# Sums of weight blocks on GpSimd replaced by accumulating DMAs, and the order of the token-half sums changed

## Chip, cores and metric

One core of a Trainium2 chip runs the kernel. The metric is the device time of one execution in microseconds (us); of several runs the median counts. HW below is 512 columns of fp32, half a weight unit of 128x1024; such a half over 128 partitions is 256 KB.

## What is computed

One step of a trunk of four layers over 640 tokens (512 of group ii and 128 of group i), width 1024, all fp32. Each layer is a token mixer (short convolution, pooling, attention, short convolution) followed by a SwiGLU feed-forward with hidden width 2816:

```python
def swiglu(h, w_in, w_out):
    g, u = jnp.split(h @ w_in, 2, axis=-1)
    return (jax.nn.silu(g) * u) @ w_out
...
        xp = xp + mod_p[5] * swiglu(hp, ffn_in_w[i], ffn_out_w[i])
        xs = xs + mod_s[5] * swiglu(hs, ffn_in_w[i], ffn_out_w[i])
```

## The kernel before

**Precision.** Every fp32 product is made of three fp32r ones: a value is kept as a high and a low part, and PE (TensorE) adds hi x hi, hi x lo and lo x hi. ACT (ScalarE) makes the high part of a weight unit by a copy to w_hi (line 1203; line 1253 for half units), DVE (VectorE) the low part by subtracting it from the raw weights (line 1701; line 1821). The order of work is written out by hand on each engine, with semaphores between them.

**Loads.** SP (SyncE) loads weight units of 128x1024 into the four rows of `raw`, one DMA of 512 KB each (line 443), as soon as the low part of the unit that lay there is made. POOL (GpSimd) loads modulation weights in layers 0 to 2 by its own DMA queue (line 542), none in layer 3.

**The feed-forward of layer 3.** The hidden tiles are taken in chunks of 8, 8 and 6. A hidden tile needs one gate unit and one up unit: a pair. In layers 0 to 2, and for the first two pairs of layer 3, a unit is multiplied plainly (lines 704, 705; `h_unit`, `ffn_in_quad`). For the other 6 + 8 + 6 = 20 pairs of layer 3 `seven_chunk` is used: tokens are halved (320 and 320 columns, two more for the shift), the feature dimension is halved, and gate and up make the third split, so eight half-size products are due; seven are made instead (Winograd's form of Strassen's scheme), of sums of weight blocks and sums of token halves. One product p1 to p7 is 4 feature tiles x 3 passes = 12 matmuls of 128x322 (line 757). Products come in the order of `_order`: p1, p5, p2, p6, p3, p7 for the first pair, then p1 of the next pair, p4 of the last, p5, p6, p2, p7, p3. After a chunk the 8 output units of the down projection follow (lines 704, 705).

**Block homes.** w_hi and w_lo hold four half units; a block is split into the home of the block four (at a few places three) before it, once the product of that one is through (`REFILL`). So ACT's `refill` (block_hi, line 1253) stands directly behind its wait for a product: in `after_p5` ahead of the copy out of PSUM that PE's p3 waits for (p5_kept, line 1299), in `after_p1` and `after_p6` behind the copies that p6 and p7 wait for (p1_kept, line 1292; u2_kept, line 1303). On DVE `after_p3` adds p3 (line 1883), multiplies by rinv (line 1886) and splits a block, `after_p7` adds p7 (line 1904), for which PE's p4 waits (c22_out).

**Sums of weight blocks.** POOL makes four a pair with tensor operations (`s13`, `s2`, `s4`; lines 591, 595, 601, 608). Blocks 1, 2 and 4 are halves of the raw weights; 5 is the sum s1 in s1_home, which is row 2 of tmp; 7, 6 and 3 are differences that overwrite halves of `raw` in place, so POOL waits until DVE has made the low part of block 1 (line 595) and of block 2 (line 608) of that pair.

**Sums of token halves.** POOL makes them once, for four feature tiles k = 0 to 3: t1_of (lines 556 to 558) and t234_of (lines 566 to 571). ACT and DVE split them: `t1_hi_of`, `t2_hi_of` (line 1266), `t3_hi_of` (line 1269), `t4_hi_of` (line 1274), and t1_lo (line 1834), t2_lo (line 1840), t3_lo (line 1844), t4_lo (line 1848). The order on POOL is t1 of all k, t234 of k = 0 and 1, then s13 and s2 of the first pair, and between s2 and s4 of it t234 of k = 2 and 3. On ACT and DVE the splits of t2 are spread over the four units of the plain quad (`T2_ROWS`), and those of t3 follow at the start of `seven_chunk`.

**Around the first product.** In the last plain quad, `ffn_in_quad` takes a unit out of PSUM (line 1775 bias copy, line 1777 product with rinv), multiplies by the gate (line 1788), and ACT makes the high part of the hidden row (line 1215), DVE the low one (line 1715). The first four blocks of a chunk are split within units 2 and 3 of it (`first_blocks`).

```python
def after_p1(p):
    act.wait_ge(product_ready, r + p - 1)
    done(p, 1)
    act.activation(gate_row(p)[:, 0:TA], bank_x(p)[:, 0:TA], ACT.Copy).then_inc(p1_kept, 1)
    refill(p, 1)
def after_p5(p):
    done(p, 5)
    refill(p, 5)
```

Of the kernel before, what the change touches and what calls it, by code (L numbers as in the profile page):

```python
# [18 lines left out]
F32 = mybir.dt.float32  # L19
# [153 lines left out]
def build(nc, d):  # L173
    with ExitStack() as ctx:
# [99 lines left out]
        s_made = sem("s_made")  # L274
# [118 lines left out]
        s1_home = tmp[:, 2, 0:HW]  # L393

        def block_source(p, m):

            j = 2 * (p % 2)
            return {1: raw[:, j, 0:HW], 6: raw[:, j, 0:HW], 2: raw[:, j, HW:2 * HW], 3: raw[:, j, HW:2 * HW],
                    7: raw[:, j + 1, 0:HW], 4: raw[:, j + 1, HW:2 * HW], 5: s1_home}[m]
# [21 lines left out]
        def _(sp):  # L421
# [17 lines left out]
            def load(q, tiles, units=range(4)):  # L439
                for j in units:  # L440

                    sp.wait_ge(w_lo_ready, 4 * q + (j - 3))
                    sp.dma_start(raw[:, j, 0:tiles * P], d["weights"][4 * q + j, :, 0:tiles * P]).then_inc(raw_in[j], 16)

# [35 lines left out]
            for layer in range(DEPTH):  # L480
# [33 lines left out]
                with sp.Fori(0, 2 * (Q_IN + Q_OUT)) as i:  # L514
                    load(i + q, KD)
                q += 2 * (Q_IN + Q_OUT)
                with sp.Fori(0, Q_LAST) as i:
                    load(i + q, KD)
                q += Q_LAST
# [11 lines left out]
        def _(pool):  # L531
# [45 lines left out]
            def s13(layer, c, p, q, n):  # L577

                first, j, qq = _pairs_before(layer, c), 2 * (p % 2), q + p // 2
# [3 lines left out]
                if p == 0 and c == 0:  # L583

                    pool.wait_ge(sum_ready, 2 * layer + 2)
                elif p:

                    pool.wait_ge(block_lo_ready, SEVEN * first + PLACE[n][p - 1, 5] + 1)
                elif c > FIRST_SEVEN[layer]:
                    pool.wait_ge(block_lo_ready, SEVEN * first)  # L590
                pool.tensor_tensor(s1_home, up_w[:, 0:HW], up_w[:, HW:2 * HW], ALU.add).then_inc(s_made, 1)

                pool.wait_ge(block_lo_ready, SEVEN * first + PLACE[n][p, 1] + 1)
                pool.wait_ge(s_made, 4 * (first + p) + 1)
# [2008 lines left out]
```

## Time and profile before

| | |
|---|---|
| median of 3 runs | 2645.55 us (2645.55 to 2646.04) |
| the profiled execution's own time | 2645.6 us |
| its span in the trace | 2643.9 us |
| mean granted clock of PE | 0.997 |
| busy: PE, DVE, ACT, POOL | 99%, 70%, 34%, 9% |
| seven-product stage of layer 3 | from 2216.2 us to about 2590 us of the span |

The span is that of the instructions; the execution's time has 1.7 us more around it. All places in the trace are counted from the span's start. PE is the matmul engine; an entry "<-ACT tmp L1292" behind an idle time names what ended it. A time to landing runs from a DMA's issue to its semaphore. Matmuls are pipelined, so each shows about 0.31 us though they begin 0.15 us apart.

### The profile page before, as it was taken

The numbers are of one execution on the slowest core, as the hardware profiler recorded it, in microseconds if no ns is written. First come the engines' busy times: TensorE is split into PE (matmuls) and PEld (weight loads), VectorE is DVE, ScalarE is ACT, GpSimd is POOL, SyncE is SP. The second block draws the span as 40 slices with busy tenths as digits, with TensorE's granted clock in tenths as the row PEclk, the third lists the DMA queues.
The fourth block names the chain that finished last, engine by engine and source line by source line (L and its number), as shares of the span: only waits on it lengthen the run. The fifth ranks groups of instructions, "written<-read, shape, count | busy, mean of one in ns | idle before, by whom it ended". The sixth has DMA issues, their size and how long they took to land.

```text
span 2643.9 us, 45052 instructions
## 1 busy us (share of the span) xinstructions
PE 2623.6 (99%) x17398; PEld 2553.1 (97%) x17398; DVE 1851.8 (70%) x3097; ACT 888.7 (34%) x1330; POOL 249.5 (9%) x297
## 2 busy tenths in 40 slices
PE   9999999999999999999999999999999998999998
PEld 5999999999999999999967999999999998999998
DVE  5888778676586776846675668777375557849486
ACT  4223331222342222124675431221242234425253
POOL 0000000000000000000000000000000025324040
PEclk9999999999999999999999999999999999999999
DMA  7444335444223443422101234434122221212222
GB/s 301 152 143 141 130 128 175 135 152 143 77 77 128 156 154 127 158 65 80 51 13 73 88 127 159 151 123 156 62 82 73 78 72 48 104 56 86 91 76 76
DMA packets 85625, 295.19 MB, mean 112 GB/s; under 512 B 10112, under 2 KB 13312, under 8 KB 85248
## 3 DMA queue, kind: packets, MB, share of 16 engines
q1 hardware_dynamic: 60016, 200.74, 22.6%
q0 software_dynamic: 25488, 92.81, 10.9%
q8 instruction: 79, 1.29, 0.2%
q14 instruction: 42, 0.34, 0.0%
HBM read 290.63 MB, written 2.88 MB: 111 GB/s over the span
## 4 chain that ended last, share of the span: by engine, by line
PE 93%; DVE 4%; issue 1%; ACT 1%; DMA 1%; POOL 0%; SPq 0%; DVEq 0%; ACTq 0%; POOLq 0%
PE ps L704 40%; PE ps L705 40%; PE ps L757 6%; PE ps_x L1003 1%; PE ps_sum L757 1%; PE ps L979 1%; PE ps_sum L990 1%; DMA mix<-in_ada_head 1%; DVE w_lo L1821 1%; PE ps L1135 1%; PE ps L1086 0%; DVE w_lo L1701 0%; PE ps L860 0%; ACT w_hi L1203 0%; DVE tmp L1916 0%
## 5 line engine op out<-in xcount | busy, mean ns | idle before, releaser
L1701 DVE TENSOR_TENSOR w_lo<-raw,w_hi 128x1024 fp32r<-128x1024 f32 (+2 forms) x319 | 381.0, 1194 | 463.5 <-ACT w_hi L1203 462.2
L1203 ACT ACTIVATE w_hi<-raw 128x1024 fp32r<-128x1024 f32 (+2 forms) x319 | 329.3, 1032 | 915.0 <-PE ps L705 903.1
L704 PE MATMUL ps<-h_hi,w_hi 128*128 128x320 f32 x1568 | 490.0, 313 | 0.7 <-DVE h_lo L2014 0.7
L705 PE MATMUL ps<-h_lo,w_hi 128*128 128x322 f32 x1568 | 488.5, 312 | 0.0
L704 PE MATMUL ps<-h_lo,w_hi 128*128 128x320 f32 x1568 | 487.3, 311 | 0.0
L705 PE MATMUL ps<-h_hi,w_lo 128*128 128x322 f32 x1568 | 487.3, 311 | 0.0
L704 PE MATMUL ps<-h_hi,w_lo 128*128 128x320 f32 x1568 | 487.0, 311 | 0.0
L705 PE MATMUL ps<-h_hi,w_hi 128*128 128x322 f32 x1568 | 486.0, 310 | 0.0
L1729 DVE CUSTOM_DVE_ANT_0 ps_x<-ada_w,cond 128x1024 f32<-128x1024 f32 x354 | 435.8, 1231 | 33.5 <-DVE tmp L1777 13.0
L705 PEld LDWEIGHTS ps<-h_hi,w_hi 128*128 128x128 f32 x1568 | 297.2, 190 | 0.6
L705 PEld LDWEIGHTS ps<-h_hi,w_lo 128*128 128x128 f32 x1568 | 297.3, 190 | 0.0
L704 PEld LDWEIGHTS ps<-h_hi,w_hi 128*128 128x128 f32 x1568 | 295.6, 189 | 1.4 <-DVE h_lo L2014 0.8
L704 PEld LDWEIGHTS ps<-h_hi,w_lo 128*128 128x128 f32 x1568 | 296.5, 189 | 0.0
L705 PEld LDWEIGHTS ps<-h_lo,w_hi 128*128 128x128 f32 x1568 | 295.6, 189 | 0.0
L704 PEld LDWEIGHTS ps<-h_lo,w_hi 128*128 128x128 f32 x1568 | 294.4, 188 | 0.0
L704 PE MATMUL ps<-g_hi,w_hi 128*128 128x320 f32 x884 | 274.3, 310 | 0.4
L705 PE MATMUL ps<-g_hi,w_lo 128*128 128x320 f32 x884 | 273.2, 309 | 0.0
L704 PE MATMUL ps<-g_hi,w_lo 128*128 128x320 f32 x884 | 273.1, 309 | 0.0
L705 PE MATMUL ps<-g_hi,w_hi 128*128 128x320 f32 x884 | 273.1, 309 | 0.0
L705 PE MATMUL ps<-g_lo,w_hi 128*128 128x320 f32 x884 | 273.1, 309 | 0.0
L704 PE MATMUL ps<-g_lo,w_hi 128*128 128x320 f32 x884 | 273.1, 309 | 0.0
L542 POOL DMA_DIRECT2D ada_w<-in_ada_w x177 | 93.8, 530 | 1730.1 <-DVE ada_raw L1729 1351.9
(237 smaller groups left out, 4090.4 us busy)
## 6 DMA issues: line engine op xcount, KB each, us to landing
raw<-in_weights SPq DMA_DIRECT2D x323, 512.0 KB, 3.5
ada_w<-in_ada_w POOLq DMA_DIRECT2D x177, 512.0 KB, 3.8
raw<-in_weights SPq DMA_DIRECT2D x32, 384.0 KB, 3.0
mix<-in_ada_head SPq DMA_DIRECT2D x16, 512.0 KB, 10.5
x<-in_x SPq DMA_DIRECT2D x8, 320.0 KB, 10.1
out_y<-mix SPq DMA_DIRECT2D x16, 160.0 KB, 2.0
mix<-in_spread SPq DMA_DIRECT2D x1, 1088.0 KB, 7.6
cond<-in_cond SPq DMA_DIRECT2D x1, 1024.0 KB, 14.7
```

Source lines behind the costliest of these rows:

```text
L542: pool.dma_start(ada_w[:, j * D:(j + 1) * D], d["ada_w"][ADA_N * qa + (j - LEAD)]).then_inc(ada_in[j], 16)
L704: pe.matmul(ps[:, 2 * slot, 0:TA], w[:, slot, ws], a(k)[:, 0:TA], start=begin, stop=end)
L705: mm = pe.matmul(ps[:, 2 * slot + 1, 0:width - TA], w[:, slot, ws], a(k)[:, TA:width], start=begin, stop=end)
L757: mm = pe.matmul(out, w[:, ws], a[:, k, :], start=begin and k == 0 and i == 0, stop=k == HALF - 1 and i == 2, skip_group_check=True)
L979: pe.matmul(out[:, 0:TS], row[:, qt * P:(qt + 1) * P], key[:, 0:TS], start=True, stop=True)
L990: mm = pe.transpose(sum_flat[:, k * P:(k + 1) * P], tmp[:, n % 2, k * P:(k + 1) * P], ident[:])
L1003: pe.matmul(ps_rot, val, of_sample[:, k, :], start=(k == 0), stop=(k == 4))
L1135: mm = pe.matmul(head_row[g % 2], cond_k[:, 2 * pair + k, :], head_w[:, n % HEAD_SLOTS, k * HEAD_W * P:(k + 1) * HEAD_W * P], start=(pair ...
L1203: act.activation(w_hi[:, j % 2, 0:tiles * P], raw[:, j, 0:tiles * P] if src is None else src, ACT.Copy).then_inc(w_hi_ready, 1)
L1701: dve.tensor_tensor(w_lo[:, j % 2, 0:tiles * P], raw[:, j, 0:tiles * P] if src is None else src, w_hi[:, j % 2, 0:tiles * P].bitcast(F32), ...
L1729: dve.tensor_tensor_reduce(ada_products, ada_w[:, j * D:(j + 1) * D], cond[:, v, :], 1.0, 0.0, ALU.mult, ALU.add, ada_raw[:, j, v:v + 1]). ...
L1821: dve.tensor_tensor(block_home(w_lo, n, b), block_source(p, m), block_home(w_hi, n, b).bitcast(F32), ALU.subtract).then_inc(block_lo_ready, 1)
```

## The change

Each sum of weight blocks is begun by a plain load from HBM into a home and finished by accumulating DMAs (source and destination in SBUF) from POOL's queue; s1 and s2 have homes in the two rows of `rope`, which layer 3 does not use, s4 in row 2 of tmp, and s3 is added into the up half of `raw`. Each DMA has a semaphore of its own. Since all sums are now additions, s2, s3 and s4 have the other sign; t1, t2 and t4 are split with a factor of -1, and the up row is scaled by -1 and subtracted from. SP issues two raw loads and three home loads a pair, in one written-out order; POOL issues five accumulating DMAs a pair. On POOL all four t234 stand ahead of the first pair's sums. The splits of t2 and t4 change as the one of t1 shown here.

```diff
-        s1_home = tmp[:, 2, 0:HW]
+        s1_home, s2_home, s4_home = rope[:, 0, 0:HW], rope[:, 1, 0:HW], tmp[:, 2, 0:HW]
         def block_source(p, m):
             j = 2 * (p % 2)
-            return {1: raw[:, j, 0:HW], 6: raw[:, j, 0:HW], 2: raw[:, j, HW:2 * HW], 3: raw[:, j, HW:2 * HW],
-                    7: raw[:, j + 1, 0:HW], 4: raw[:, j + 1, HW:2 * HW], 5: s1_home}[m]
+            return {1: raw[:, j, 0:HW], 2: raw[:, j, HW:2 * HW], 4: raw[:, j + 1, HW:2 * HW], 7: raw[:, j + 1, 0:HW],
+                    5: s1_home, 6: s2_home, 3: s4_home}[m]
...
+            def load_pair(layer, c, q, p):
+                first, place, j, qq = _pairs_before(layer, c), PLACE[SEVENS[c]], 2 * (p % 2), q + p // 2
+                load(qq, KD, (j, j + 1))
+                gate_w, up_w = d["weights"][4 * qq + j], d["weights"][4 * qq + j + 1]
+                def free(m):
+                    if p:
+                        sp.wait_ge(block_lo_ready, SEVEN * first + place[p - 1, m] + 1)
+                    elif first:
+                        sp.wait_ge(block_lo_ready, SEVEN * first)
+                free(5)
+                sp.dma_start(s1_home, up_w[:, 0:HW]).then_inc(s1_in, 16)
+                free(6)
+                sp.dma_start(s2_home, up_w[:, HW:2 * HW]).then_inc(s2_in, 16)
+                free(3)
+                if p == 0 and c == FIRST_SEVEN[layer]:
+                    sp.wait_ge(sum_ready, 2 * layer + 2)
+                sp.dma_start(s4_home, gate_w[:, HW:2 * HW]).then_inc(s4_in, 16)
...
-                with sp.Fori(0, 2 * (Q_IN + Q_OUT)) as i:
+                plain = min(FIRST_SEVEN[layer], 2) * (Q_IN + Q_OUT)
+                if FIRST_SEVEN[layer] == 0:
+                    plain += PLAIN_PAIRS // 2
+                with sp.Fori(0, plain) as i:
                     load(i + q, KD)
-                q += 2 * (Q_IN + Q_OUT)
-                with sp.Fori(0, Q_LAST) as i:
-                    load(i + q, KD)
-                q += Q_LAST
+                q += plain
+                for c in range(FIRST_SEVEN[layer], 3):
+                    for p in range(SEVENS[c]):
+                        load_pair(layer, c, q, p)
+                    q += SEVENS[c] // 2
+                    if c < 2:
+                        with sp.Fori(0, Q_OUT) as i:
+                            load(i + q, KD)
+                        q += Q_OUT
+                if FIRST_SEVEN[layer] == 3:
+                    with sp.Fori(0, Q_LAST) as i:
+                        load(i + q, KD)
+                    q += Q_LAST
...
-            def s13(layer, c, p, q, n):
-                first, j, qq = _pairs_before(layer, c), 2 * (p % 2), q + p // 2
+            def sums_of_pair(layer, c, p, q):
+                made, j, qq = 16 * (_pairs_before(layer, c) + p + 1), 2 * (p % 2), q + p // 2
                 gate_w, up_w = raw[:, j, :], raw[:, j + 1, :]
                 pool.wait_ge(raw_in[j], 16 * qq + 16)
                 pool.wait_ge(raw_in[j + 1], 16 * qq + 16)
-                if p == 0 and c == 0:
-                    pool.wait_ge(sum_ready, 2 * layer + 2)
-                elif p:
-                    pool.wait_ge(block_lo_ready, SEVEN * first + PLACE[n][p - 1, 5] + 1)
-                elif c > FIRST_SEVEN[layer]:
-                    pool.wait_ge(block_lo_ready, SEVEN * first)
-                pool.tensor_tensor(s1_home, up_w[:, 0:HW], up_w[:, HW:2 * HW], ALU.add).then_inc(s_made, 1)
-                pool.wait_ge(block_lo_ready, SEVEN * first + PLACE[n][p, 1] + 1)
-                pool.wait_ge(s_made, 4 * (first + p) + 1)
-                pool.tensor_tensor(up_w[:, 0:HW], gate_w[:, 0:HW], up_w[:, 0:HW], ALU.subtract).then_inc(s_made, 1)
-            def s2(layer, c, p):
-                first, gate_w = _pairs_before(layer, c), raw[:, 2 * (p % 2), :]
-                pool.wait_ge(s_made, 4 * (first + p) + 2)
-                pool.tensor_tensor(gate_w[:, 0:HW], s1_home, gate_w[:, 0:HW], ALU.subtract).then_inc(s_made, 1)
-            def s4(layer, c, p, n):
-                first, gate_w = _pairs_before(layer, c), raw[:, 2 * (p % 2), :]
-                pool.wait_ge(block_lo_ready, SEVEN * first + PLACE[n][p, 2] + 1)
-                pool.wait_ge(s_made, 4 * (first + p) + 3)
-                pool.tensor_tensor(gate_w[:, HW:2 * HW], gate_w[:, HW:2 * HW], gate_w[:, 0:HW], ALU.subtract).then_inc(s_made, 1)
-            def begin_chunk(layer, c, q, n, turns):
-                s13(layer, c, 0, q, n)
-                s2(layer, c, 0)
-                if turns:
-                    t234_of(layer, 2)
-                    t234_of(layer, 3)
-                s4(layer, c, 0, n)
-            def rest_of_chunk(layer, c, q, n, triples):
-                for p in range(1, n):
-                    if p % 2 == 1 and p > 1 and p // 2 < len(triples):
+                pool.dma_start(up_w[:, 0:HW], gate_w[:, 0:HW], accum_op=ALU.add).then_inc(s3_made, 16)
+                pool.wait_ge(s1_in, made)
+                pool.dma_start(s1_home, up_w[:, HW:2 * HW], accum_op=ALU.add).then_inc(s1_made, 16)
+                pool.wait_ge(s3_made, made)
+                pool.wait_ge(s2_in, made)
+                pool.dma_start(s2_home, up_w[:, 0:HW], accum_op=ALU.add).then_inc(s2_made, 16)
+                pool.wait_ge(s4_in, made)
+                pool.dma_start(s4_home, up_w[:, 0:HW], accum_op=ALU.add).then_inc(s4_half, 16)
+                pool.wait_ge(s4_half, made)
+                pool.dma_start(s4_home, up_w[:, HW:2 * HW], accum_op=ALU.add).then_inc(s4_made, 16)
+            def sums_of_chunk(layer, c, q, n, triples):
+                for p in range(n):
+                    if p % 2 == 1 and p // 2 < len(triples):
                         ada_triple(triples[p // 2])
-                    s13(layer, c, p, q, n)
-                    s2(layer, c, p)
-                    s4(layer, c, p, n)
+                    sums_of_pair(layer, c, p, q)
...
-                    t234_of(layer, 0)
-                    t234_of(layer, 1)
+                    for k in range(HALF):
+                        t234_of(layer, k)
...
-                    begin_chunk(layer, c, qc, tiles, c == FIRST_SEVEN[layer])
-                    if triples and not (kind == "attn" and c == 0):
-                        ada_triple(triples[0])
-                    rest_of_chunk(layer, c, qc, tiles, triples)
+                    sums_of_chunk(layer, c, qc, tiles, triples)
...
-                    act.wait_ge(s_made, 4 * (first + p) + {5: 1, 7: 2, 6: 3, 3: 4}[m])
+                    act.wait_ge({5: s1_made, 6: s2_made, 7: s3_made, 3: s4_made}[m], 16 * (first + p + 1))
...
-                act.activation(t1_hi[:, k, :], t2_full[:, k, :], ACT.Copy).then_inc(t_hi_ready, 1)
+                act.activation(t1_hi[:, k, :], t2_full[:, k, :], ACT.Identity, scale=-1.0).then_inc(t_hi_ready, 1)
...
-                dve.tensor_tensor(t1_lo[:, k, :], t2_full[:, k, :], t1_hi[:, k, :].bitcast(F32), ALU.subtract).then_inc(t_lo_ready, 1)
+                dve.scalar_tensor_tensor(out=t1_lo[:, k, :], in0=t2_full[:, k, :], scalar=-1.0, in1=t1_hi[:, k, :].bitcast(F32),
+                                         op0=ALU.mult, op1=ALU.subtract).then_inc(t_lo_ready, 1)
...
-                    dve.tensor_tensor(up_row(p)[:, 0:TA], bank_x(p)[:, 0:TA], rinv[:, 0:TA], ALU.mult).then_inc(c21_out, 1)
+                    dve.scalar_tensor_tensor(out=up_row(p)[:, 0:TA], in0=bank_x(p)[:, 0:TA], scalar=-1.0, in1=rinv[:, 0:TA],
+                                             op0=ALU.mult, op1=ALU.mult).then_inc(c21_out, 1)
...
-                    dve.tensor_tensor(up_row(p)[:, TA:T], up_row(p)[:, TA:T], rinv[:, TA:T], ALU.mult).then_inc(up_scaled, 1)
+                    dve.scalar_tensor_tensor(out=up_row(p)[:, TA:T], in0=up_row(p)[:, TA:T], scalar=-1.0, in1=rinv[:, TA:T],
+                                             op0=ALU.mult, op1=ALU.mult).then_inc(up_scaled, 1)
...
-                                                     op0=ALU.add, op1=ALU.mult)
+                                                     op0=ALU.subtract, op1=ALU.mult)
```

## Rows read from the trace of the kernel before

**Rows 1.** The page, busy time, share of the span and instructions of each engine.
```profile
PE 2623.6 (99%) x17398; PEld 2553.1 (97%) x17398; DVE 1851.8 (70%) x3097; ACT 888.7 (34%) x1330; POOL 249.5 (9%) x297
```
**Rows 2.** Waits of PE from 2000 us on: total, times, longest.
```profile
PE ps L757 <- ACT tmp L1292: 5.6, 1, 5.6
PE ps_sum L757 <- DVE w_lo L1821: 1.1, 1, 1.1
```
**Rows 3.** Stretches: busy of PE, PEld, DVE, ACT, POOL; clock; DMA share; GB/s.
```profile
2228.70:2234.00 5.30, 5.30 (x20) 5.30 (x21) 5.30 (x12) 4.22 (x10) 2.03 (x1) 0.50 0.01 3
...
2232.00:2308.00 76.00, 76.00 (x506) 75.88 (x506) 68.65 (x104) 38.62 (x71) 29.84 (x19) 0.99 0.28 98
```
**Rows 4.** Timeline of PE: start, duration, instruction (idle before it).
```profile
2201.99 0.31 PE L704 MATMUL ps<-h_hi,w_hi 128*128 128x320 f32 x1
...
2216.23 0.31 PE L757 MATMUL ps<-h_hi,w_hi 128*128 128x322 f32 x1
...
2236.58 0.31 PE L757 MATMUL ps<-h_hi,w_hi 128*128 128x322 f32 x1
...
2238.37 0.41 PE L757 MATMUL ps<-turned,w_hi 128*128 128x322 f32 x1
```
**Rows 5.** Timeline of POOL around the first pair of sums.
```profile
2198.54 1.29 POOL L591 TENSOR_TENSOR tmp<-raw 128x512 f32<-128x512 f32 x1 [5.12 <-DMA raw<-in_weights]
2210.74 1.67 POOL L595 TENSOR_TENSOR raw<-raw 128x512 f32<-128x512 f32 x1 [10.91 <-DVE w_lo L1821]
...
2213.74 0.89 POOL L566 TENSOR_TENSOR mix<-h_hi,h_lo 128x322 f32<-128x322 f32 x1
...
2223.05 0.86 POOL L571 TENSOR_TENSOR mix<-mix 128x322 f32<-128x322 f32 x1
```
**Rows 6.** Timeline of ACT from the first blocks to the copy for PE.
```profile
2209.84 0.61 ACT L1253 ACTIVATE w_hi<-tmp 128x512 fp32r<-128x512 f32 x1
...
2216.59 0.47 ACT L1266 ACTIVATE turned<-mix 128x322 fp32r<-128x322 f32 x1 [3.47 <-POOL mix L568]
...
2225.77 0.74 ACT L1215 ACTIVATE g_hi<-tmp 128x640 fp32r<-128x640 f32 x1 [7.66 <-DVE tmp L1788]
...
2228.22 0.41 ACT L1292 ACTIVATE tmp<-ps 128x320 f32<-128x320 f32 x1
```
**Rows 7.** Timeline of DVE over the same stretch.
```profile
2193.50 1.21 DVE L1701 TENSOR_TENSOR w_lo<-raw,w_hi 128x1024 fp32r<-128x1024 f32 x1
...
2199.23 1.68 DVE L1701 TENSOR_TENSOR w_lo<-raw,w_hi 128x1024 fp32r<-128x1024 f32 x1
...
2200.90 0.81 DVE L1777 TENSOR_TENSOR tmp<-ps,tmp 128x640 f32<-128x640 f32 x1
...
2205.87 1.01 DVE L1788 SCALAR_TENSOR_TENSOR tmp<-tmp,bias 128x512 f32<-128x512 f32 x2
...
2218.61 1.06 DVE L1840 TENSOR_TENSOR turned<-mix,turned 128x322 fp32r<-128x322 f32 x1 [6.55 <-POOL mix L571]
2219.59 2.64 DVE L1821 TENSOR_TENSOR w_lo<-raw,w_hi 128x512 fp32r<-128x512 f32 x2
...
2223.07 2.67 DVE L1788 SCALAR_TENSOR_TENSOR tmp<-tmp,bias 128x512 f32<-128x512 f32 x2
...
2233.43 0.68 DVE L1821 TENSOR_TENSOR w_lo<-raw,w_hi 128x512 fp32r<-128x512 f32 x1
```
**Rows 8.** Groups by form, 2100 to 2644 us: busy, mean ns.
```profile
L1821 DVE TENSOR_TENSOR w_lo<-tmp,w_hi 128x512 fp32r<-128x512 f32 x20 | 13.7, 683 | 0.0
L1253 ACT ACTIVATE w_hi<-tmp 128x512 fp32r<-128x512 f32 x20 | 12.6, 630 | 17.5 <-PE ps L757 16.4 <-POOL raw L595 1.1
```
**Rows 9.** DMA issues from 300 to 900 us: KB each, median us to landing.
```profile
raw<-in_weights SPq DMA_DIRECT2D x73, 512.0 KB, 3.6
ada_w<-in_ada_w POOLq DMA_DIRECT2D x62, 512.0 KB, 3.8
...
raw<-in_weights SPq DMA_DIRECT2D x4, 256.0 KB, 2.5
```

More of the change, by code:

```diff
@@ L273, in build @@
         t_lo_ready = sem("t_lo_ready")
-        s_made = sem("s_made")
+        s1_in = sem("s1_in")
+        s2_in = sem("s2_in")
+        s4_in = sem("s4_in")
+        s4_half = sem("s4_half")
+        s1_made = sem("s1_made")
+        s2_made = sem("s2_made")
+        s3_made = sem("s3_made")
+        s4_made = sem("s4_made")
         block_hi_ready = sem("block_hi_ready")
@@ L667, in _ @@
                     turn_rows(layer)
-                    t234_of(layer, 0)
-                    t234_of(layer, 1)
+                    for k in range(HALF):
+                        t234_of(layer, k)
                 for c in range(FIRST_SEVEN[layer], 3):
@@ L1261, in t1_hi_of @@
                 act.wait_ge(t1_made, HALF * LAYER_T[layer] + k + 1)
-                act.activation(t1_hi[:, k, :], t2_full[:, k, :], ACT.Copy).then_inc(t_hi_ready, 1)
+                act.activation(t1_hi[:, k, :], t2_full[:, k, :], ACT.Identity, scale=-1.0).then_inc(t_hi_ready, 1)
             def t2_hi_of(layer, k):
                 act.wait_ge(t2_made, HALF * LAYER_T[layer] + k + 1)
-                act.activation(t2_hi[:, k, :], t2_full[:, k, :], ACT.Copy).then_inc(t_hi_ready, 1)
+                act.activation(t2_hi[:, k, :], t2_full[:, k, :], ACT.Identity, scale=-1.0).then_inc(t_hi_ready, 1)
             def t3_hi_of(layer, k):
@@ L1273, in t4_hi_of @@
                 act.wait_ge(t_lo_ready, T_STEPS * LAYER_T[layer] + 2 * HALF + k + 1)
-                act.activation(t4_hi[:, k, :], t4_full[:, k, :], ACT.Copy).then_inc(t_hi_ready, 1)
+                act.activation(t4_hi[:, k, :], t4_full[:, k, :], ACT.Identity, scale=-1.0).then_inc(t_hi_ready, 1)
             def seven_chunk(layer, c, q, n, r, g, tiles):
@@ L1839, in t2_lo_of @@
                 dve.wait_ge(t4_made, HALF * LAYER_T[layer] + k + 1)
-                dve.tensor_tensor(t2_lo[:, k, :], t2_full[:, k, :], t2_hi[:, k, :].bitcast(F32), ALU.subtract).then_inc(t_lo_ready, 1)
+                dve.scalar_tensor_tensor(out=t2_lo[:, k, :], in0=t2_full[:, k, :], scalar=-1.0, in1=t2_hi[:, k, :].bitcast(F32),
+                                         op0=ALU.mult, op1=ALU.subtract).then_inc(t_lo_ready, 1)
             def t3_lo_of(layer, k):
@@ L1847, in t4_lo_of @@
                 dve.wait_ge(t_hi_ready, T_STEPS * LAYER_T[layer] + 3 * HALF + k + 1)
-                dve.tensor_tensor(t4_lo[:, k, :], t4_full[:, k, :], t4_hi[:, k, :].bitcast(F32), ALU.subtract).then_inc(t_lo_ready, 1)
+                dve.scalar_tensor_tensor(out=t4_lo[:, k, :], in0=t4_full[:, k, :], scalar=-1.0, in1=t4_hi[:, k, :].bitcast(F32),
+                                         op0=ALU.mult, op1=ALU.subtract).then_inc(t_lo_ready, 1)
             def seven_chunk(layer, c, q, n, pr, g, tiles, ada):
```

## The prediction

> **What bounds the kernel now.** The page comes first. PE is busy for 2623.6 of the span's 2643.9 us [rows 1], so no change off PE can give back more than PE's idle time plus what PE does at a lower clock. Next the waits of PE, from 2000 us on, which hold layer 3, the only layer with sums of weight blocks: one wait of 5.6 us for ACT's copy at line 1292 and one of 1.1 us for DVE's low part of a block [rows 2]. Both lie where the seven-product stage begins. The table of stretches then shows the second price of that gap: in 2228.7 to 2234.0 PE works at a granted clock of 0.50, the lower of its two levels, 1.2 instead of 2.4 GHz [rows 3]. Twenty matmuls took 5.3 us there; at 12 in 1.79 us they take 3.0, so 2.3 us went. In the stretch of the first chunk, 2232 to 2308, PE is never idle [rows 3], and the same holds for the later chunks, for which the waits list nothing. The whole prize is therefore 5.6 + 1.1 + 2.3 = 9.0 us; measured on the timeline, the second pair's first product begins at 2236.58, and six products of 1.79 us behind 2216.23 would put it at 2226.97, so 9.6 us [rows 4]. That is the most the change can win.
>
> **Where the gap comes from.** POOL's timeline: it stood idle 5.12 us for raw weights, made one sum at 2198.54, then waited 10.91 us for DVE's low part of the block it was to overwrite, and only after two more sums began the token-half sums of k = 2 and 3, of which the last began at 2223.05 [rows 5]. ACT waited 3.47 us for them at 2216.59, then 7.66 us for DVE before line 1215 at 2225.77, and its copy for PE ran at 2228.22 [rows 6]. DVE lost 6.55 us at 2218.61 for the same sums; its two block splits at 2219.59 took 2.64 us and the two products of line 1788 took 2.67 us at 2223.07, where 1.01 us was enough at 2205.87 with POOL idle [rows 7].
>
> **Part 1, token sums first.** t234 of k = 2, 3 needs only rows of h and of t1_lo, which exist when POOL falls idle at 2193.4. The same ten operations then run from there to about 2204 (10.2 us for the pair of k in [rows 5], 2213.7 to 2223.9). The first chain of ACT and DVE moves as follows. The last plain product ends at 2216.2; ACT splits two blocks at 0.63 each, DVE follows at 0.68 each, to 2218.4; bias copy and line 1777 take 0.9 (0.81 for the latter, [rows 7]) to 2219.4; line 1788 takes 1.0, to 2220.4. So ACT's line 1215 begins at 2220.4 and not at 2225.77, 5.4 us earlier, and with it the copy that PE waits for, which ends at 2223.3. PE, three products behind 2216.23, is there at 2221.6: a gap of 1.7 us stays. Before, the clock went down inside a gap of 5.6 us; I take it not to fall in one of 1.7 us, since the gap of 1.1 us before it left the clock up. From there: ACT's work between that copy and line 1303 is unchanged, about 0.2 us late for the seventh product; the fourth product of pair 0 waits for DVE's chain of lines 1883, 1886, 1821 and 1904, about 2.6 us (a block split at 0.68, a product over the whole row at 0.9, two half as wide at 0.5, after the 0.81 of line 1777), and that begins when the last block split before it is through, which ended at 2234.1 [rows 7] and now ends 5.4 us earlier, at 2228.7. So the fourth product starts near 2231.35 where it was at 2238.37 [rows 4]. That is **7.0 us** won.
>
> What that order costs: in 2193.5 to 2204 POOL now works beside DVE. The weight split at 2199.23, which had a POOL sum beside it, took 1.68 us, the one at 2193.50 alone 1.21 [rows 7]: 0.5 more for it, and 0.4 for the short split behind it, 0.9 in all on the way to line 1777, which ended 0.28 us ahead of the unit that needs its bank, at 2201.99 [rows 4, 7]. So 0.6 us is lost (0 to 2). The Trainium skill, SBUF — State Buffer, "Who interferes with whom", has it that the two share one read interface held for a whole instruction; by that each of the three DVE operations could wait out a POOL one, and the loss would be near 2 us, the gain 5.
>
> **Part 2, the sums as DMAs.** Removed: 80 POOL operations of 1.3 to 1.7 us; none was waited for by PE in steady state, so this alone is worth nothing on PE. DVE's splits from raw no longer share the time with POOL and come down to the 0.68 us that those from tmp take [rows 8]; worth nothing either, since PE has no gap there, and it is cover for what follows. Changing the sign in the token splits and in the two products keeps the number and size of operations: nothing. Added: three plain loads of 256 KB per pair on SP and five accumulating DMAs of 256 KB on POOL, 60 and 100 in all. The issue costs on SP hold nothing up: each raw load of the next pair waits for the block m = 4, which is split after blocks 5, 6 and 3 for which the new loads wait.
>
> The critical loop is s4_home, single and written by a load and two adds in a row. Block 3 of pair p is split on ACT (0.63) and DVE (0.68) [rows 8], SP loads the home anew (2.5 us, the 256 KB row [rows 9]), POOL adds twice. With 0.1 for hops the loop takes 3.9 + 2A, A being one accumulating DMA from issue to landing. A pair gives 7 x 1.79 = 12.5 us. No row shows A. From below: a plain 256 KB load, 2.5. From above: two POOL transfers one behind the other, 2 x 3.8 = 7.6 [rows 9]. I take **3.8**: 256 KB more cost 1.1 us on SP (3.6 against 2.5), the second operand is 256 KB more, and POOL's queue is 0.2 above SP's; the row is that of one 512 KB transfer of POOL. The loop is then 11.5 us, inside 12.5, and nothing is lost.
>
> How far does it hold? Counted from the chunk's first product, ACT wants s4 of pair 1 at 16.1 us, of pair p at 16.1 + 12.5(p - 1); it may stand still for 2 x 1.79 - 0.63 - 2 x 0.41 (the split and two copies of the length in [rows 6]) = 2.1 us before PE's seventh product notices. s4 of pair 1 is made at 5.8 + 2A, later ones each 3.9 + 2A behind. The last pair of eight: 29.2 + 14A against 93.2; of six: 21.4 + 10A against 68.2. So A up to 4.57 costs nothing; beyond it the three chunks lose (14A - 64.0) + 2(10A - 46.8). The first sums are no trouble: s1 of pair 0 is begun at 2204.7 and made at 2208.5, ACT took that block at 2209.84 [rows 6]; s2 by 2212.5, wanted at 2217.
>
> **Sum.** The profiled execution took 2645.6 us (0.05 above the median of the three runs), 2645.6 - 7.0 + 0.6 = **2639.2 us**. What a measurement of this kernel can tell from no change is 0.2%, 5.3 us, so the forecast is only just faster.
>
> **Rivals.** (1) The s4 loop decides, slower than before. Place: PE's seventh and third products wait for ACT, which stands at s4_made. It costs from A = 4.57 on and turns the sign at 4.82; A = 5 loses 12.4 (2651.6), 5.8 loses 39.6 (2679), 7.6 loses 100.8 (2740). For it: the adding path was never seen here, two adds stand in a row in a loop with 1.0 us spare, and raw loads for the next pair start while s4 is being added. Against: A needs 0.8 us more than the nearest row.
> (2) The opening gap closes only in part: POOL beside DVE costs more, or ACT's copy still comes more than 3 us late and the clock falls again (2.3 us). Gain 1 to 5, about 2642.5. For: ACT and DVE have no slack in that stretch.
> (3) The DMA engines fill up. 7.43 MB went in 76 us at a share of 0.28 [rows 3], 2.86 us per MB at full share. Per pair 1.05 MB raw is 3.0 us, 0.79 MB of loads 2.2, five adds 3.7 if they move like copies: 9 of 12.5. If each byte added costs double, 7.5 and 12.7 in all, just above 12.5: 0.2 us per pair over 17 pairs, some 4 us, 2643, and more where transfers queue. The Trainium skill, Collectives: The Full Stack, "The bandwidth ceiling: the fold count and why AG ≠ RS ≠ AR", states just this: an add reads two sources and runs at half the copy's rate. No run here shows it yet.
>
> **Chances.** Forecast 0.43, all faster. Rival 1 0.30 (0.27 slower, 0.03 within 0.2%). Rival 2 0.17, within 0.2%. Rival 3 0.10, half within, half slower. Faster 0.43, same 0.25, slower 0.32. The range reaches down to the whole prize (2636) and up to A = 5.8 (2680). Cases of both signs hold much of the chance: the forecast's own range is 2636 to 2641.
>
> **What would show it.** Right: POOL without tensor operations from about 2204, PE's wait for line 1292 down to 1 to 3 us, granted clock 1.00 around 2228, accumulating DMAs at about 3.8 us to landing, DVE's splits at 0.68, DMA share near 0.7 in the chunks. Wrong: ACT's splits from s4_home waiting for DMA and PE waiting for ACT in each pair from the third or fourth of a chunk on, or landing times above 4.6 us.

## The result, and the profile after

The changed kernel takes **2673.66 us** (median of 5 runs, 2671.71 to 2676.25) against 2645.55 before: a ratio of 1.0107, 95% interval 1.0096 to 1.0118, so **28.1 us slower**. The forecast was 2639.2, faster; the time lies inside the stated range, on the side of rival 1. The profiled execution took 2672.69 us, its span 2670.7, 1.0 below the median.

One correction to the description of the change: the sums s2, s3 and s4 are all plain sums there, and it is the factor of -1 on t1, t2, t4 and on the up row that makes up for it. No cost hangs on it.

From the page of the changed kernel: the busy line (of before in [rows 1]) and the DMA issues (KB each, median us to landing).

```profile
PE 2633.2 (99%) x17398; PEld 2559.0 (96%) x17398; DVE 1801.6 (67%) x3097; ACT 883.8 (33%) x1330; POOL 216.4 (8%) x317
...
rope<-in_weights SPq DMA_DIRECT2D x40, 256.0 KB, 4.5
rope<-raw POOLq DMA_DIRECT2D x40, 256.0 KB, 4.4
tmp<-raw POOLq DMA_DIRECT2D x40, 256.0 KB, 5.0
tmp<-in_weights SPq DMA_DIRECT2D x20, 256.0 KB, 2.8
```

The span grew by 26.8 us in two parts. PE's idle time (span less busy) went from 20.3 to 37.5, 17.2 more; its busy time from 2623.6 to 2633.2, 9.6 more for the same 17398 matmuls. The waits of PE from 2000 us on name the first part; of before they are [rows 2] (the copy of line 1292 is line 1305 now, that of line 1303 is line 1316, the split of line 1253 is line 1266):

```profile
PE ps L770 <- ACT tmp L1316: 23.1, 13, 4.2
PE ps L770 <- ACT tmp L1305: 1.4, 1, 1.4
...
PE ps L717 <- DVE w_lo L1714: 0.4, 1, 0.4
PE ps L717 <- DVE tmp L1790: 0.2, 1, 0.2
```

The wait that the change was to shorten did shrink, from 5.6 to 1.4. But a new one, for the copy that p7 waits for, comes 13 times. The waits of ACT tell why that copy is late: on ACT it stands behind the split of block 3, which `after_p5` makes ahead of both copies (lines 1312 and 1316) and whose source is s4_home.

```profile
ACT w_hi L1266 <- DMA tmp<-raw: 71.2, 16, 7.2
...
ACT w_hi L1266 <- DMA rope<-raw: 18.1, 10, 2.9
```

The second part shows in stretches of 4 us (columns as in [rows 3]). Before, a stretch of 8 us from 2394 on held 55 matmuls at clock 1.00. Now:

```profile
2224.00:2228.00 4.00, 4.00 (x27) 3.88 (x28) 4.00 (x9) 4.00 (x11) 0.00 (x0) 1.00 0.50 115
...
2392.00:2396.00 4.00, 0.25 (x2) 0.00 (x0) 0.27 (x1) 0.93 (x3) 2.26 (x3) 0.95 0.78 132
2396.00:2400.00 4.00, 3.59 (x13) 3.60 (x14) 2.95 (x6) 2.02 (x5) 1.56 (x2) 0.50 0.85 178
```

Behind the shortened gap of the opening the clock holds at 1.00, where it was 0.50 behind the long one [rows 3]. After PE has stood still at 2392 it is granted half: 13 matmuls take 3.59 us where 0.15 each would be 1.9. Nine stretches of 4 us between 2268 and 2576 are below 1.00; their busy time less 0.15 per matmul adds up to 6.2 us. So a long stall can be paid twice, as the opening gap was before, but not every one was: behind the stalls of 2.42, 2.46, 2.91 and 4.16 us the clock was below 1.00, behind two of 2.60 and 2.62 us (2298.18, 2427.21) it stayed at 1.00, and the runs don't say what decides. The rest (9.6 and the 2.3 that the opening no longer costs, less 6.2) I can't place; part of it is that the first matmul behind a wait shows as 0.4 to 0.6 us.

**One round in which PE loses, and one in which it doesn't.** From the timelines of SP, POOL, ACT and PE in the changed kernel. L450 loads raw units, L472 loads s4_home, L632 and L635 are s4's two adds.

```profile
2268.82 0.33 SPq L472 DMA_DIRECT2D tmp<-in_weights  x1
2271.96 0.85 POOL L632 DMA_DIRECT2D tmp<-raw  x1 [1.95 <-DMA tmp<-in_weights]
2273.71 0.82 SPq L450 DMA_DIRECT2D raw<-in_weights  x2
2275.52 0.85 POOL L635 DMA_DIRECT2D tmp<-raw  x1 [2.71 <-DMA tmp<-raw]
2280.47 0.63 ACT L1266 ACTIVATE w_hi<-tmp 128x512 fp32r<-128x512 f32 x1 [1.55 <-DMA tmp<-raw]
...
2379.09 0.33 SPq L472 DMA_DIRECT2D tmp<-in_weights  x1
2381.44 1.00 SPq L450 DMA_DIRECT2D raw<-in_weights  x2
2382.72 0.85 POOL L632 DMA_DIRECT2D tmp<-raw  x1 [1.95 <-DMA tmp<-in_weights]
2391.66 0.85 POOL L635 DMA_DIRECT2D tmp<-raw  x1 [8.09 <-DMA tmp<-raw]
2395.07 0.63 ACT L1266 ACTIVATE w_hi<-tmp 128x512 fp32r<-128x512 f32 x1 [7.18 <-DMA tmp<-raw]
2396.41 0.64 PE L770 MATMUL ps<-h_hi,w_hi 128*128 128x322 f32 x1 [4.16 <-ACT tmp L1316]
```

In the first round the first add is through after 3.6 us (2271.96 to 2275.52). In the second it takes 8.9, POOL stands still for it, ACT waits 7.18 us for the finished sum, and PE 4.16 us for ACT. What differs is the place of the two raw loads, 1 MB in all: 1.75 us after the first add there, 1.28 us before it here. (SP issues the home loads of s1 and s2 behind the raw loads, here at 2383.69 and 2386.36, so they move with them.) Of the 20 first adds 19 have raw loads near them (times from the add's issue to that of the second). With the raw loads issued between 1.4 us ahead of the add and 0.3 us behind it, 13 adds take 5.5 to 8.9 us; with 0.8 us behind it, two take 4.4 and 5.7; with 1.0 us or more, four take 3.6 to 4.1. The two lines from 2200 to 2600 us, which hold 19 of the 20 pairs, from the view of one source line:

```profile
L632 POOL DMA_DIRECT2D tmp<-raw x19: 844/852/1190, 2209.1 to 2586.2; - x19
...
DMA to landing us min/median/max: 3.3/5.9/8.7
...
L635 POOL DMA_DIRECT2D tmp<-raw x19: 844/847/854, 2214.0 to 2590.2; - x19
...
DMA to landing us min/median/max: 3.3/3.5/7.7
```

Both move 256 KB into the same home: 3.3 us at best, and 5.9 or 3.5 in the median by what else is in flight. The loop is read off SP's timeline, first and last reload of s4_home in the steady part of each chunk:

```profile
2239.88 0.33 SPq L472 DMA_DIRECT2D tmp<-in_weights  x1
...
2281.85 0.33 SPq L472 DMA_DIRECT2D tmp<-in_weights  x1
...
2363.76 0.33 SPq L472 DMA_DIRECT2D tmp<-in_weights  x1
...
2457.77 0.33 SPq L472 DMA_DIRECT2D tmp<-in_weights  x1
...
2537.15 0.33 SPq L472 DMA_DIRECT2D tmp<-in_weights  x1
...
2597.01 0.33 SPq L472 DMA_DIRECT2D tmp<-in_weights  x1
```

Three, six and four rounds take 42.0, 94.0 and 59.9 us: 15.1 us a pair on average, where PE needs 12.5.

**What an add costs the DMA engines.** From 2200 to 2620 us queue q0 holds the 100 adds and nothing else, queue q1 the plain loads (packets, MB, share of 16 engines):

```profile
q0 software_dynamic: 14400, 26.22, 36.9%
q1 hardware_dynamic: 16733, 45.26, 33.6%
```

36.9% of 420 us over 100 adds is **1.55 us each**; the plain loads beside them come to 0.82 us for each 256 KB (0.77 before, same stretch), so an add takes the engines **about twice as long as a copy**. The same sum for the kernels below that make all sums by DMA gives 1.53 to 1.61. In e8 only five adds run, from 2204 to 2222 us and at a share of 0.58, and they come to 1.52: it is the add and hardly the crowd. A pair asks for five adds (7.75) and, in raw units and home loads, seven times 256 KB (5.74), 13.5 us of engines against PE's 12.5. The stretch 2240 to 2260 has the DMA share at 0.97; before the first chunk's was 0.28 [rows 3].

```profile
2240.00:2260.00 20.00, 19.01 (x127) 18.74 (x128) 15.03 (x28) 10.03 (x20) 5.98 (x7) 1.00 0.97 225
```

### The profile page after: what moved, and what is told of

Same layout as the page of the kernel before. It is cut to its first block and busy times, and to the rows that moved or that the text cites. A ratio compares the mean times of both kernels' runs of the same rounds, so it can differ in the third digit from the quotient of the medians.

```text
span 2670.7 us, 44972 instructions
## 1 busy us (share of the span) xinstructions
PE 2633.2 (99%) x17398; PEld 2559.0 (96%) x17398; DVE 1801.6 (67%) x3097; ACT 883.8 (33%) x1330; POOL 216.4 (8%) x317
```

## Experiments

Two theories. **Load**: an add takes the engines twice as long as a copy, the engines fill, whatever flies together delays each other, and s4's two adds in a row, in a loop through one home, turn that into waits of PE. **Latency**: the loop is too long by the adding path's own time, whatever the traffic. A third question is where the gain of the opening went, and whether the DMAs had any part in it. The expectations count an add at 1.48 us, a home load at 0.67 and a raw load at 1.27, an early reading that gave 12.0 us a pair where the sum above gives 13.5. "Before" in these runs was 2645.70 to 2645.81.

| kernel | us | to before | PE idle | PE busy |
|---|---|---|---|---|
| before | 2645.55 | | 20.3 | 2623.6 |
| after | 2673.66 | +28.1 | 37.5 | 2633.2 |
| e1 order alone | 2642.09 | -3.7 | 18.3 | 2621.7 |
| e2 after, old order | 2676.61 | +30.8 | 41.8 | 2632.3 |
| e3 two homes for s4 | 2664.0 | +18.2 | 34.0 | 2630.4 |
| e4 one add for s4 | 2667.01 | +21.2 | 33.1 | 2630.5 |
| e6 all homes double | 2660.17 | +14.4 | 29.6 | 2626.2 |
| e5 one add, all homes double | 2651.16 | +5.4 | 21.6 | 2626.9 |
| e7 quarter s1 | 2666.84 | +21.0 | 32.3 | 2631.2 |
| e10 as e5, quarter s1 | 2644.4 | -1.3 | 19.6 | 2622.2 |
| e11 raw loads later | 2700.44 | +54.7 | 56.2 | 2642.0 |
| e9 own homes, no DMA sums | 2640.44 | -5.3 | 16.1 | 2622.5 |
| e8 as e9, first pair by DMA | 2640.47 | -5.3 | 16.5 | 2622.4 |
| e8b as e9, two pairs by DMA | 2639.95 | -5.8 | 16.7 | 2621.7 |

### e1: the order alone, in the kernel before

```diff
                 s2(layer, c, 0)
-                if turns:
-                    t234_of(layer, 2)
-                    t234_of(layer, 3)
                 s4(layer, c, 0, n)
...
-                    t234_of(layer, 0)
-                    t234_of(layer, 1)
+                    for k in range(HALF):
+                        t234_of(layer, k)
```

> The kernel before with only the order on POOL changed: all four t234 ahead of the first pair's sums, which stay tensor operations. The prediction's first part alone: its opening gap goes from 5.6 + 1.1 us to about 1.5 to 2 us and the clock stays up there, so 2639 to 2640 us (7.0 won, 0.6 lost beside POOL, the sums made by POOL a little slower than DMAs). Rival: the order alone brings little, because the in-place sums then come late and ACT waits for them instead: 2643 us or more, with a wait of PE above 3 us in the opening.

2642.09 us, ratio 0.9986 (0.9977 to 0.9995): 2.1 above the range expected, 0.9 below the rival's. PE's waits (L1289 is the copy of line 1292, L1901 the adding of p7 of line 1904):

```profile
PE ps L754 <- ACT tmp L1289: 2.6, 1, 2.6
PE ps L754 <- DVE tmp L1901: 1.7, 1, 1.7
```

and from its DVE timeline a split that takes 0.68 without POOL beside it [rows 8]:

```profile
2232.08 1.75 DVE L1818 TENSOR_TENSOR w_lo<-tmp,w_hi 128x512 fp32r<-128x512 f32 x1
```

The clock no longer falls, though the gap stays 2.6 us instead of 1.4 (PE busy is 1.9 us less), and p4 waits: POOL's sums of weight blocks, now later, run beside DVE in the critical stretch (line 601 from 2231.55 for 1.74 us) and slow it. ACT also waits 3.7 us for that late sum, as the rival had it. Moving the order alone brings a little over half of what it brings with POOL silent.

### e2: the old order, in the changed kernel

```diff
-                    for k in range(HALF):
-                        t234_of(layer, k)
+                    t234_of(layer, 0)
+                    t234_of(layer, 1)
...
+                if turns:
+                    t234_of(layer, 2)
+                    t234_of(layer, 3)
                 pool.wait_ge(s4_half, made)
```

> The changed kernel with the old place of t234 of k = 2 and 3, between the two adds into the first pair's s4. Both theories of the loss (loop through s4_home, full DMA engines) leave the chunks as they are; the opening gap comes back, so 5 to 8 us more than the changed kernel's 2673, 2678 to 2681 us. If instead the opening is what costs, it would be below 2673.

2676.61 us, 1.0116 (1.0101 to 1.0132), 2.9 above after where 5 to 8 were expected. With the old order the loss is all still there, so the new one has no part in it. Undoing the order costs less than the 6.4 us that part 1 was thought to be worth, since without tensor sums of blocks ahead of it POOL reaches the two token sums at once, 10 us sooner than the 2213.74 of [rows 5]:

```profile
2203.50 1.52 POOL L607 TENSOR_TENSOR mix<-h_hi,h_lo 128x322 f32<-128x322 f32 x1
```

### e3 and e6: more homes

In e3 s4 has a second home, a third of `ada_w`, by turns; in e6 s1 and s2 have one too, and every semaphore of a sum is double.

```diff
-        s1_home, s2_home, s4_home = rope[:, 0, 0:HW], rope[:, 1, 0:HW], tmp[:, 2, 0:HW]
+        s1_home, s2_home = rope[:, 0, 0:HW], rope[:, 1, 0:HW]
+        s4_homes = [tmp[:, 2, 0:HW], ada_w[:, 0:HW]]
...
-                free(3)
+                if p >= 2:
+                    sp.wait_ge(block_lo_ready, SEVEN * first + place[p - 2, 3] + 1)
```

> The changed kernel with two homes for s4, taken in turn, so that the load and both adds of a pair no longer wait for the split of the pair before; traffic is unchanged. Loop theory (the home is the bound, a round of load, two adds and split took 14.1 us against the 12.5 of a pair): the waits of PE for line 1316 go, 2640 to 2645 us. DMA theory (at 1.48 us an add, 0.67 a home load and 1.27 a raw load the engines need 12.0 of 12.5 us a pair): nothing of substance changes, adds land in 5 us and more, 2660 to 2673 us.

> The changed kernel, five adds a pair, with two homes for each of s1, s2 and s4. The need is 12.0 of 12.5 us a pair plus some queueing. DMA theory: close to the run with two homes for s4 alone, 2658 to 2666 us, DMA share above 0.9 in the chunks. Loop theory (s2_home's and s1_home's rounds took over there): 2645 us or less.

e3 2664.0 us, 1.0066 (1.005 to 1.0081); e6 2660.17, 1.0057 (1.0042 to 1.0071). Both lie in the range of the load theory. Freed of its home's turn, the loop through s4_home should have lost nothing if it alone decided. A third of the loss goes with e3, half with e6, and in e6 the engines are nearly full:

```profile
2240.00:2290.00 50.00, 45.06 (x299) 44.24 (x299) 33.66 (x63) 23.70 (x47) 14.99 (x18) 1.00 0.94 226
```

The DMA share is 0.94 over 50 us (0.95 in 2370 to 2430), and PE still waits 14.6 us for the same copy. But e6 keeps a second loop, which no home lifts: POOL's own order. Each pair it stands still for the landing of s3's add and for that of s4's first add, one behind the other:

```profile
2390.41 1.19 POOL L628 DMA_DIRECT2D ada_w<-raw  x1
2397.76 0.84 POOL L631 DMA_DIRECT2D ada_w<-raw  x1 [6.17 <-DMA ada_w<-raw]
...
2403.00 0.85 POOL L626 DMA_DIRECT2D rope<-raw  x1 [2.64 <-DMA raw<-raw]
2403.54 1.19 POOL L628 DMA_DIRECT2D tmp<-raw  x1
```

That round takes 13.1 us (2390.41 to 2403.54) without a wait for raw weights or a home; 13.8 is the mean of three rounds from 2241.46 to 2282.95. With both landings at the quiet 3.3 to 3.5 us it would take about 9 (an estimate). So the chain comes from the order and its length from the load, and e6 can't tell full engines from this loop. No run changed POOL's order, with s4's second add behind the next pair's first ones.

### e4 and e5: one add for s4

s4 = gate2 + s2, with s2_home as the source: four adds a pair instead of five. SP reloads s2_home only once s4 is made. e4 has single homes, e5 those of e6.

```diff
                 free(6)
+                if first + p:
+                    sp.wait_ge(s4_made, 16 * (first + p))
                 sp.dma_start(s2_home, up_w[:, HW:2 * HW]).then_inc(s2_in, 16)
...
-                pool.dma_start(s4_home, up_w[:, 0:HW], accum_op=ALU.add).then_inc(s4_half, 16)
-
-                pool.wait_ge(s4_half, made)
-                pool.dma_start(s4_home, up_w[:, HW:2 * HW], accum_op=ALU.add).then_inc(s4_made, 16)
+                pool.wait_ge(s2_made, made)
+                pool.dma_start(s4_home, s2_home, accum_op=ALU.add).then_inc(s4_made, 16)
```

> The changed kernel with s4 made by one add of s2_home instead of two adds (four adds a pair, not five); s2_home is then free for its next load only when s4 is made. The home's round is now load, add of s2, add of s4, without the split. DMA theory: the engines need 10.5 of 12.5 us, adds land in about 4 us and most of the loss goes, 2640 to 2650 us. Loop theory with unchanged landing times (load 2.8, adds 4.4 and 5.0, hops 0.5: 12.7 us): a small loss of 0.2 us per pair stays, 2643 to 2650 us; the two differ in the landing times, about 4 against 4.4 to 5.0 us.

> One add for s4 (four adds a pair) and two homes for each of s1, s2 and s4, so no home's round is left that could bind; the engines need 2.54 + 2.0 + 4 x 1.48 = 10.5 of 12.5 us a pair. If serial rounds through single homes are the loss in the run with one add, 2640 to 2645 us. If queueing in well filled DMA engines is it, adds still land in 5 us and more and 2650 us or more stay.

e4 2667.01 us, 1.0092 (1.0077 to 1.0108); e5 2651.16, 1.0022 (1.0013 to 1.0031). e5 is in the load theory's range; e4 is 17 us above both, which had priced the round through s2_home with landings of 4 to 5 us. With single homes the wait only changes its name:

```profile
PE ps L770 <- DVE w_lo L1834: 16.9, 10, 2.8
```

and ACT waits 67.2 us for rope<-raw, s2's home, whose round now holds a load and two adds in a row, as s4's did. With homes enough, one add less is worth 9.0 us (e5 against e6), 0.53 us for each of the 17 pairs behind a chunk's first, and the DMA share in 2224 to 2300 falls from 0.84 to 0.72.

### e7 and e10: less traffic at the same structure

s1's load and add take 128 of the 512 columns; the rest of s1_home keeps old values, so block 5 is not the sum. e7 does it in the changed kernel, e10 in e5.

```diff
-                sp.dma_start(s1_home, up_w[:, 0:HW]).then_inc(s1_in, 16)
+                sp.dma_start(s1_home[:, 0:P], up_w[:, 0:P]).then_inc(s1_in, 16)
...
-                pool.dma_start(s1_home, up_w[:, HW:2 * HW], accum_op=ALU.add).then_inc(s1_made, 16)
+                pool.dma_start(s1_home[:, 0:P], up_w[:, HW:HW + P], accum_op=ALU.add).then_inc(s1_made, 16)
```

> The changed kernel with the load of s1 and the add into it cut to 128 of their 512 columns, so three quarters of the sum s1 are not made; every instruction, wait and home round stays, only (0.67 + 1.48) x 3/4 = 1.6 us of the engines' time per pair goes. DMA theory: adds land sooner and a good part of the 28 us comes back, 2652 to 2662 us. Loop theory with landing times as they are: 2670 to 2674 us.

> One add for s4, two homes for each of s1, s2 and s4, and the load of s1 and its add cut to 128 of 512 columns (three quarters of the sum s1 are not made). The engines need 8.9 of 12.5 us a pair and no home's round binds. If traffic is all that is left of the loss in the run with one add and two homes (2651.2), this comes to the level of the opening's gain, 2639 to 2643 us. If adds through POOL's queue stay late for another reason, 2646 us or more.

e7 2666.84 us, 1.008 (1.0062 to 1.0097); e10 2644.4, 0.9996 (0.9987 to 1.0005). s1 is hardly on the path (in after ACT waits 3.7 us for its add, and POOL 11.8 us for its home load ahead of a longer wait for s4's), and s4's adds are untouched; cutting it by three quarters brings 6.8 us in the one and 6.8 in the other. s4's adds land a little sooner in e7 (tmp<-raw in its DMA issues, 2200 to 2620 us, against 5.0 in after):

```profile
tmp<-raw POOLq DMA_DIRECT2D x40, 256.0 KB, 4.5
```

That is a median over two unlike groups. Line by line, s4's first add stays near its 5.7 (5.6), while POOL's wait for it falls from 101.9 to 96.6 us in all and s3's add lands 0.5 us sooner (4.1 to 3.6). In e10 s4's add doesn't land sooner than in e5 (median 5.2 against 4.7). Neither run is where a theory had it: e7 lies between the ranges (load 2652 to 2662, latency 2670 to 2674), e10 between 2643 and 2646. A time that falls with traffic off the path is what load predicts and latency alone doesn't, but the load theory had the size too large, and through which transfers the 6.8 us come is not shown.

### e11: the raw loads moved behind the first add

```diff
                 first, place, j, qq = _pairs_before(layer, c), PLACE[SEVENS[c]], 2 * (p % 2), q + p // 2
+                if p > 1:
+                    sp.wait_ge(s4_half, 16 * (first + p))
                 load(qq, KD, (j, j + 1))
```

> The changed kernel with one wait more on SP: from the third pair of a chunk on, the two raw loads of the next pair (1 MB) are issued only when the first of s4's two adds of this pair has landed. In the changed kernel that first add lands 5.9 us after its issue (median of 19, 3.3 to 8.7), the second, of the same size, 3.5. The slow ones have the raw loads issued between 1.3 us before and 0.8 us after them, those of 3.5 to 4.1 us have them at least 1 us later. Theory (the engines are shared by whatever is in flight, so an add is slow because 1 MB of raw loads runs beside it, and the sum of the work is what counts): the first add falls to about 3.5 to 4, the second rises to about 5.5 to 6.5, since the raw loads now start beside it, the two together stay near 9.5, and the time is 2668 to 2690, not faster by more than a few us. Rival A (the first add is slow because three other adds of POOL's own queue stand before it): it stays near 5.9, the second near 3.5, and the later raw loads make it 2680 or more. Rival B (only the order of the transfers was unlucky): both at about 3.5 to 4 and the time 2650 or less.

2700.44 us, 1.0207 (1.019 to 1.0224). The two source lines again, shifted by two:

```profile
L634 POOL DMA_DIRECT2D tmp<-raw x19: 844/852/1190, 2209.4 to 2611.2; - x19
...
DMA to landing us min/median/max: 3.3/3.4/7.6
...
L637 POOL DMA_DIRECT2D tmp<-raw x19: 842/847/854, 2214.1 to 2614.8; - x19
...
DMA to landing us min/median/max: 3.3/7.5/8.8
```

The delay goes where the raw loads (and the home loads of s1 and s2 behind them) go: the first add falls from 5.9 to 3.4, the second rises from 3.5 to 7.5. The three adds that stand ahead of the first in POOL's queue are there as before, so rival A falls, and so does rival B. The sum of the two medians is 10.9 where 9.5 was expected, and the time is 10 us above the range given: I had counted the later raw loads at nothing, but POOL now waits for them in most pairs (164.8 us in 16 waits, 110.5 in 9 in the changed kernel), and the round grows to 16.5 us (2241.53 to 2291.11, three rounds).

### e9, e8 and e8b: the sums by tensor operations in homes of their own

The changed kernel with POOL's `tensor_tensor` for all pairs (e9), all but the first (e8) or all but the first two (e8b). Homes, order and signs are those of the change, and the home loads fall away for those pairs. The lines are e8's; e9 raises the old semaphores in place of v1 to v4.

```diff
+                if not by_dma(layer, c, p):
...
+                    free(5)
+                    pool.tensor_tensor(s1_home, up_w[:, 0:HW], up_w[:, HW:2 * HW], ALU.add).then_inc(v1_made, 1)
...
+                    pool.tensor_tensor(up_w[:, 0:HW], gate_w[:, 0:HW], up_w[:, 0:HW], ALU.add).then_inc(v3_made, 1)
+                    free(6)
+                    pool.tensor_tensor(s2_home, s1_home, gate_w[:, 0:HW], ALU.add).then_inc(v2_made, 1)
+                    free(3)
...
+                    pool.tensor_tensor(s4_home, s2_home, gate_w[:, HW:2 * HW], ALU.add).then_inc(v4_made, 1)
```

> All 20 pairs by tensor operations of POOL into the homes s1, s2 and s4, none by DMA, token sums first. Against the run with only the order changed it tells what the in-place waits cost; against the one with the first pair by DMA, what POOL beside DVE costs in the opening. In the chunks PE waits for nothing in either. If the opening's waits (2.6 and 1.7 us there) come from the late in-place sums, 2640 to 2641 us; if they come from POOL slowing DVE, 2642 us as there.

> Only the first pair of layer 3 by accumulating DMAs, where the engines are nearly idle; the other 19 by tensor operations of POOL, written into the homes s1, s2 and s4, so that they need not wait until blocks 1 and 2 are split. Token sums first. No loss in the chunks, since POOL's four operations take 6 to 7 of 12.5 us, and the opening of the changed kernel, whose wait of PE was 1.4 us: 2638.5 to 2639.5 us, 2.5 to 3.5 below the run with the order alone. Rival: DVE, slowed again by POOL next to it, lets p4 of the first pair wait as in that run, 2641 to 2642 us.

> As the run with the first pair by accumulating DMAs, but the first two pairs. POOL then makes no tensor operation between 2204 us and the third pair, so DVE's products and splits in the opening are not slowed (1.35 us for its line of 1.01, 1.39 for one of 0.68): 0.3 to 1 us less than that run, 2639.5 to 2640.2 us. Rival: the second pair's adds meet the raw loads of pairs 3 and 4 and come late, as in the changed kernel, 2641 us or more.

e9 2640.44 us, 0.998 (0.9971 to 0.9989); e8 2640.47, 0.998 (0.9971 to 0.9989); e8b 2639.95, 0.9978 (0.9969 to 0.9987). e9 and e8b came as expected, e8 1.0 above its range and below its rival's. Waits of PE in e8b, beside the 0.4 and 0.2 of the plain quad:

```profile
PE ps L798 <- ACT tmp L1336: 1.4, 1, 1.4
PE ps L798 <- DVE w_lo L1865: 0.8, 2, 0.7
```

Own homes bring 1.6 us more than e1's order, as e9's expectation had it for late in-place sums; I put that down to sums that no longer wait for the low part of a block they overwrite, which no run took apart from the rest. DMAs for the first pair bring nothing over e9, for the first two pairs 0.5 us more at most (the ranges 2639.48 to 2641.06 and 2640.01 to 2640.93 overlap). e8b has the lowest time of all measured, 5.8 us below before.

## Why the prediction was wrong

**The opening: right, nearly to the number.** Foretold were a gap of 1.7 us before the copy, no fall of the clock, 0.6 us lost to POOL beside DVE. The waits above show 1.4, clock 1.00, and 0.4 + 0.2. From PE's timeline of the changed kernel:

```profile
2216.96 0.31 PE L770 MATMUL ps<-h_hi,w_hi 128*128 128x322 f32 x1
...
2223.93 0.56 PE L770 MATMUL ps<-turned,w_hi 128*128 128x322 f32 x2 [1.44 <-ACT tmp L1305]
...
2231.50 0.57 PE L770 MATMUL ps<-turned,w_hi 128*128 128x322 f32 x2
```

p4 of pair 0 begins at 2231.50; 2231.35 + 0.6 were foretold, and 2238.37 is of before [rows 4]. So 6.9 us were won there. Rival 2 fell with it, as did the harsher price that I had drawn from the Trainium skill, SBUF — State Buffer, "Who interferes with whom": the loss was 0.6 and not 2. But the slowing was real, DVE's timeline has the split of [rows 7] that took 1.21 us alone at 1.89 beside POOL:

```profile
2193.17 1.89 DVE L1714 TENSOR_TENSOR w_lo<-raw,w_hi 128x1024 fp32r<-128x1024 f32 x1
```

What it hit was hardly waited for. DVE's splits from raw came down from 875 to 691 ns (0.68 foretold), worth nothing on PE, as foretold.

**The step that failed: "I take 3.8" for A.** It was one number for both adds, from the row of a 512 KB load with nothing said of its company. An add without raw loads beside it lands in 3.3 to 3.5 us, so for that the value was even on the high side; but beside 1 MB of raw loads it lands in 7.4 (2255.98 and 2256.62 to 2264.02, or the 7.5 of e11), and in the loop the first add meets them in most pairs: SP reloads s4_home when block 3 is split and the raw units when the block behind it is, 2.3 us later (2379.09, 2381.44), while the add follows the reload by 2.8 to 3.6 (2382.72). The formula was sound: 3.9 + 0.3 for the longer load (2.8 and not 2.5) + 3.5 + 7.4 = 15.1, the round measured. With 15.1 - 3.9 = 11.2 for 2A, A = 5.6, its terms (14A - 64.0) + 2(10A - 46.8) give 14.4 + 18.4 = 32.8 us of loss; lost beside the 6.9 won were 35.0. So rival 1 was the outcome, by the mechanism of rival 3: an add takes 1.55 us of the engines against 0.82 for a copy beside it. The Trainium skill, Collectives: The Full Stack, "The bandwidth ceiling: the fold count and why AG ≠ RS ≠ AR", says of the adds of a collective between cores that two reads make them run at half the rate of a copy, and the trace agrees for these adds within one SBUF. I priced rival 3 by a balance of means (12.7 of 12.5 us, some 4 us lost; measured 13.5) and left its effect on A out. The landings grew with what was in flight (e11), so the load set the size of rival 1. Had the two been put together, slower would have been the likelier side. Without any home's turn, e6 still loses 21.3 of the 35.0 us, by full engines or by POOL's order; the single homes add 13.7.

**A term not in the sum:** behind four of the six stalls of over 2 us in the chunks the clock was below 1.00, 6.2 us of PE time here. The prediction counted this price from [rows 3] for the opening and not for rival 1.

**The signs named for a wrong forecast came true:** ACT's splits from s4_home wait for DMA, PE waits in most pairs (from 2239.83 on, sooner than the third or fourth of a chunk), landings above 4.6 us, DMA share 0.82 in 2224 to 2300 and not near 0.7.

**What stays open.** e10, with four adds and quarter s1, is 4.0 us above e9, 3.5 of it idle PE time; its share is 0.67 and its s4 still comes late three times. That fits transfers in line in bursts, but no run showed it. How much of e6's loss is full engines and how much POOL's order is open too. Whether the loop would hold with e5's homes and the raw loads spread in halves was not tried.

## What to carry to other kernels

Price a transfer by what is in flight when it is issued, not by its landing time alone: add up the engine time of all transfers of a round (an add counted double) and, if it comes near the round itself, take for those on a serial loop the landing under load, here 7.4 us beside 1 MB of loads where a quiet one was 3.4. Look for every loop those landings stand in: a home written anew each round is one, the order of the issuing engine another. Where the engines are idle, sums made by DMAs cost nothing (e8) and brought 0.5 us at most (e8b); a tensor operation on an idle engine into a home of its own kept the gain (-5.3 us, of which the order alone gives 3.7). And a stall of PE can be paid twice, as idle time and as matmuls at the lower clock behind it: look at the granted clock behind each.

## What the runs showed of the hardware

- An accumulating DMA of 256 KB inside SBUF: 3.3 us to landing at best, 7.4 to 7.5 beside 1 MB of raw loads, and 1.52 to 1.61 us of the 16 engines, about twice the 0.77 to 0.82 of a plain load.
- Its issue shows as 0.85 us on POOL, and as 1.2 to 1.5 where several follow closely (median of L632 0.85, maximum of L626 1.53), against 0.53 for POOL's plain loads. Issues that follow closely overlap, though: L635, L624 and L626 begin at 2264.02, 2264.56 and 2265.09, so each holds the next up for 0.54 us.
- POOL beside DVE slowed the splits from 1.21 to 1.89 us and from 0.68 to 1.75, although they share no data.
- The granted clock fell behind gaps of PE of 5.6, 4.2, 2.9, 2.5 and 2.4 us and stayed at 1.00 behind others of 2.6 (twice here, once in e1) and 1.4.
